# Who multiplies the second layer's attention probabilities by their reciprocal sums: ScalarE or VectorE

## The reference, cut to what matters

```
sc = (q_lat . ckv + q_r . k_r) * HEAD_DIM ** -0.5
sc = where(valid, sc, -inf)
p  = softmax(sc)                    # exp(sc - max) / sum(exp(sc - max))
o_lat = p . ckv ;  o = o_lat . w_uv
out = concat(o) @ w_out
```

## Time and profile before

| | |
|---|---|
| median of three executions | 1579.65 us (1578.85 to 1582.76) |
| the profiled execution | 1582.23 us, its span 1580.4 us |
| PE busy | 1498.1 us (95%) |
| DVE busy | 1279.8 us (81%) |
| ACT busy | 1038.9 us (66%) |
| POOL busy | 113.9 us (7%) |
| mean granted clock of TensorE | 0.981 of full |

### The profile page before, as it was taken

One profiled execution on the slowest core, in us unless ns is written; L12 is line 12 of the kernel. 1 busy time (PEld: TensorE's weight loads), 2 busy tenths in 40 slices (PEclk: granted clock), 3 DMA queues, 4 the chain that ended last, 5 costly groups with the idle time before them and its releaser, 6 DMA issues.

```text
span 1580.4 us, 21687 instructions
## 1 busy us (share of the span) xinstructions
PE 1498.1 (95%) x7201; PEld 1164.0 (74%) x7202; DVE 1279.8 (81%) x1744; ACT 1038.9 (66%) x1357; POOL 113.9 (7%) x112
## 2 busy tenths in 40 slices
PE   3999999999898899999999999999999999999987
PEld 1645468888795478878888888888888888888865
DVE  6896458885584159989989989989989989989987
ACT  3104443443457548787887887888788788788775
POOL 5251000000000000001001001001001001001030
PEclk9999999999799899999999999999999999999999
DMA  9733967874564359999999999999999999999960
GB/s 311 267 107 137 386 253 289 318 247 172 170 214 160 107 218 395 388 347 376 385 349 380 392 353 373 393 352 374 381 370 366 386 362 368 379 371 367 391 241 28
DMA packets 209930, 482.81 MB, mean 305 GB/s; under 512 B 8084, under 2 KB 14534, under 8 KB 209750
## 3 DMA queue, kind: packets, MB, share of 16 engines
q1 hardware_dynamic: 205872, 468.91, 80.7%
q0 software_dynamic: 3360, 12.10, 2.1%
q10 hardware_dynamic: 646, 1.16, 0.2%
HBM read 474.27 MB, written 7.86 MB: 305 GB/s over the span
## 4 chain that ended last, share of the span: by engine, by line
PE 81%; ACT 5%; DVE 5%; issue 2%; DVEq 0%; ACTq 0%
PE ps L864 23%; PE ps L866 22%; PE ps L865 22%; PE ps L870 3%; DVE w_lo L2058 3%; PE ps L1399 2%; PE ps L1156 2%; ACT work L1949 1%; PE ps L1036 1%; PE ps L889 1%; ACT uT L1699 1%; ACT w_hi L1686 1%; PE ps L1067 1%; ACT uT L1708 1%; PE ps L1127 0%
## 5 line engine op out<-in xcount | busy, mean ns | idle before, releaser
L2058 DVE TENSOR_TENSOR w_lo<-ring,w_hi 128x1024 fp32r<-128x1024 f32 (+2 forms) x572 | 675.9, 1214 | 84.8 <-ACT w_hi L1686 63.7
L1686 ACT ACTIVATE w_hi<-ring 128x1024 fp32r<-128x1024 f32 (+2 forms) x572 | 595.9, 1051 | 225.4 <-PE ps L866 222.5
L864 PE MATMUL ps<-w_hi,e_hi 128*128 128x512 f32 x896 | 356.3, 398 | 5.5 <-DVE w_lo L2058 5.5
L866 PE MATMUL ps<-w_hi,e_lo 128*128 128x512 f32 x896 | 349.5, 390 | 0.0
L865 PE MATMUL ps<-w_lo,e_hi 128*128 128x512 f32 x896 | 348.8, 389 | 0.0
L2058 DVE TENSOR_TENSOR w_lo<-ring_more,w_hi 128x1024 fp32r<-128x1024 f32 x192 | 232.1, 1223 | 16.0 <-ACT w_hi L1686 7.0
L1686 ACT ACTIVATE w_hi<-ring_more 128x1024 fp32r<-128x1024 f32 x192 | 202.8, 1060 | 47.5 <-PE ps L866 47.5
L864 PEld LDWEIGHTS ps<-w_hi,e_hi 128*128 128x128 f32 x896 | 168.3, 188 | 42.0 <-DVE w_lo L2058 9.6
L866 PEld LDWEIGHTS ps<-w_hi,e_lo 128*128 128x128 f32 x896 | 168.1, 188 | 36.2
L865 PEld LDWEIGHTS ps<-w_lo,e_hi 128*128 128x128 f32 x896 | 168.5, 188 | 32.8
L864 PE MATMUL ps<-w_hi,eT_hi 128*128 128x512 f32 x448 | 176.7, 395 | 11.9 <-DVE w_lo L2058 11.9
(11 more groups left out here) (306 smaller groups left out, 1593.2 us busy)
## 6 DMA issues: line engine op xcount, KB each, us to landing
ring<-in_moe_w_gate SPq DMA_DIRECT2D x96, 1024.0 KB, 7.0
ring<-in_moe_w_up SPq DMA_DIRECT2D x80, 1024.0 KB, 6.9
ring<-in_moe_w_down SPq DMA_DIRECT2D x64, 1024.0 KB, 7.0
ring<-in_w_ada SPq DMA_DIRECT2D x24, 2048.0 KB, 12.5
ring_more<-in_moe_w_down SPq DMA_DIRECT2D x48, 1024.0 KB, 7.3
ring_more<-in_moe_w_up SPq DMA_DIRECT2D x32, 1024.0 KB, 7.5
ring_more<-in_moe_w_gate SPq DMA_DIRECT2D x16, 1024.0 KB, 7.3
ring<-in_ff_w_gate SPq DMA_DIRECT2D x5, 2048.0 KB, 7.8
```

What stands on the lines that cost most here:

```text
L864: mm(o, xh, wh, start=start, stop=False)
L866: return mm(o, xl, wh, start=False, stop=stop)
L1686: fn(w, src, ACT.Copy).then_inc(hi_ready, 1)
L2058: V.tensor_tensor(w_lo[0:n, c, 0:f], src, w_hi[0:n, c, 0:f].bitcast(F32), ALU.subtract).then_inc(lo_ready, 1)
```

## The change

`probs` is no longer called in layer 1, so ACT issues its four ACTIVATE per pair no more. Instead `weights_sum(n, True)` on DVE waits for its own reciprocal, multiplies the head's two tiles in place by the two reciprocals (`tensor_scalar`), and lets PE go itself (`p_ready`). Nobody waits for `rden_ready` in layer 1 any more. Layer 0 keeps its form.

```
@@ ACT, loop over layer 1's pairs
             for pair in range(C_HEADS // 2):
                 n = A_HEADS + 2 * pair
-                probs(n)
-                probs(n + 1)
                 if pair % 2 == 0:
                     part_out(12 + pair // 2, parts2[:, pair // 2 % 2, :], 6, (0, 0, 13, 14)[pair // 2])
                 probsT_out(n)
@@ DVE, weights_sum(n, l1)
-                V.reciprocal(rden, den).then_inc(rden_ready, 1)
+                if not l1:
+                    V.reciprocal(rden, den).then_inc(rden_ready, 1)
+                else:
+                    chained(V.reciprocal(rden, den))
+                    q = n % 3
+                    for t in range(NT):
+                        x = sm[:, q, KOFF[t]:KOFF[t] + KEYS[t]]
+                        w = V.tensor_scalar(x, x, stat[:, 24 + 2 * q + t:25 + 2 * q + t], None, ALU.mult)
+                        if t < NT - 1:
+                            step(w)
+                    w.then_inc(p_ready, 1)
```

## The result

The changed kernel took 1569.47 us (median of 4, 1568.10 to 1570.98) and the kernel before, run beside it, 1580.43 us (median of 4, 1578.85 to 1582.76). The ratio is 0.9924, 95% interval 0.9909 to 0.9938. The direction and the mechanism of the hand-over between the engines were right, the size was wrong. The profile of the changed kernel is of its fastest execution of the four (1568.10 us); the other three have none.

The account below looks back on a forecast made before the run. Bound: the ACT-PE hand-over in layer 1's attention, with ACT's multiplications a link. Terms 3.18 + 1.25 + 0.24 + 0.24 = 4.91 us; with pair 6, 5.15 to 6.58, set at 5.9: 1579.65 - 5.9 = 1573.8 us, range 1570.0 to 1577.3.

Parts of the forecast that it names:

- pair 0: Layer 1's first pair of heads, ACT the chain: from 5.64 us to 4.39, a gain of 1.25 us.
- pair 1: Layer 1 pair without a matrix-vector product: from 4.26 us to 3.66, a gain of 0.60 us.
- pairs 3, 5, 7 (order alone): Layer 1 pairs where ACT also copies a finished pair of heads: from 4.52 us to 3.66, 0.86 us each.
- pair 2: Layer 1 pair with a matrix-vector product: the small product's wait for ACT's copy goes, a gain of 0.24 us.
- pair 4: Layer 1 pair with a matrix-vector product: taken to gain the same 0.24 us as pair 2.
- pair 6: Low clock in this layer 1 pair, 524.2 to 528.0 us: 1.67 us gained if it goes, 0 if it stays.
- the price on DVE: Per head in layer 1: multiplication starts 0.20 us after the reciprocal's start, two multiplications span 0.55 us.
- The second low-clock stretch goes too: Rival, chance 0.15: low clock at pair 7's end and the product's head also vanishes, some 2.6 us; gain 9.2, time 1570.5.
- The 0.24 goes: In pair 2, the small product L903's 0.24 us wait for ACT's copy L1628 disappears; same taken for pair 4.
- Cover for what is added: DVE's next mask and maximum, pushed by 0.58 us to 3.43, stay hidden: ACT asks at 3.66, 0.23 us spare.

Follow-up runs that it names:

- the filler in the kernel before: Kernel before, ACT still multiplying, with five unused 128x128 matmuls in PE's idle time in each odd pair: ratio 0.9959, median 1578.05 us.
- The second and third profiles: Changed kernel run two more times with no edit: ratios 0.9932 and 0.9938, medians 1573.92 and 1573.27 us.
- the matrix-vector steps: Changed kernel with four steps of the next matrix-vector product moved into pairs 1, 3, 5, ahead of the first transposes: ratio 0.9928, median 1570.77 us.
- The last version: Changed kernel with four matrix-vector steps moved into pairs 1, 3, 5 and seven unused matmuls in pair 7: ratio 0.9899, median 1566.87 us.
- half on each engine: Changed kernel with each pair's first head multiplied on DVE and the second on ACT again: ratio 0.9966, median 1575.79 us.

## Why the prediction was wrong in size

Its sum, term by term, with the profiles' values, in us:

```
term                         predicted   measured
pair 0                          1.25       1.38
pair 1                          0.60       0.60
pairs 3, 5, 7 (order alone)     2.58       2.58
pair 2                          0.24       0.51
pair 4                          0.24       0.58
pair 6                       0 to 1.67     1.63  (0.57 order, 1.06 clock)
pair 7 and product, clock       0          2.49  (first profile; in the other two the stretch was there)
```

*Right.* ACT's multiplications were the link, the price on DVE was 0.20 + 0.55 per head, the odd pairs and their 3.66 us came out exactly, the head copy fell into ACT's wait, and everything behind the attention moved along unchanged. The fall of the clock in pair 6 went, as chosen.

*First failed step: "The second low-clock stretch goes too" was given 0.15 and put at nothing in the sum; it measured 2.49 us.* I argued that PE still idles between four bursts in the last pair, much as before. In the profile that stands beside the median it was gone, 1.03 us in pair 7 and 1.46 in the product, and the filler in the kernel before shows that this time is indeed the clock's, not the order's. The second and third profiles have it again. The case was neither in nor out; it should have had about half of the weight. The range reached a gain of 9.65 us (1579.65 to 1570.0), just short of the 9.77 that the stages give with it, and the measured 11.0 lies another 1.2 us beyond, which no stage holds. The choice of 5.9 halfway between 5.15 and 6.58 took 0.7 us more off a fall in pair 6 that did go.

*Second: pairs 2, 4 and 6 were mis-sized.* "The 0.24 goes" took the idle time printed before L903 as all that the wait cost. It cost 0.51 to 0.58: the row's idle time is counted from the end of the transposes, which PE overlaps with the next operation when nothing holds it (0.38 from start to start, not 0.55). In pair 4 the printed idle time was not 0.24 either but 0.34, which the prediction did not look up. Pair 0 was off by 0.13 in the same way, with operations added up at their printed lengths (0.93 from the scores to the transposes, where the trace has 0.86). Together 0.27 + 0.34 + 0.13 = 0.74, and 0.57 in pair 6 at equal clock.

*Third: the base.* The prediction subtracted from a median of three, 1579.65. Four later sets of the kernel before have medians 1583.28, 1582.02, 1582.23 and 1582.21, and the changed kernel's later medians are 1573.92 and 1573.27, beside the predicted 1573.8. That the time looks close there is luck, two errors of opposite sign: the gain, not the time, is what the steps were about.

*Cover for what is added.* The maxima were in time for ACT, as worked out, but not for PE: in pair 1 PE's scores wait 0.42 us for them. The prediction named only ACT as the one that asks. It cost nothing until the matrix-vector steps filled PE's spare time there.

*What stays open.* The ratios often give more than the stages. The stages give the changed kernel 9.8 us in its first profile and 7.1 in the other two; the ratios give 12.0, 10.8 and 9.8 us of some 1582, with intervals from 6.5 to 14.4 taken together. The last version has 16.0 (13.3 to 18.8) where its stages give 11.8. But the kernel before with filler has such a surplus too, 6.5 against 3.5, though no multiplication moved there, and over the twelve profiles of the table other than the kernel before's own two the surplus goes from -1.0 us (half on each engine) to about +4 (the last version). Each profile is one execution, the ratios go by medians, and the executions of one kernel differ by up to 8 us. So this part is not shown to belong to the change. The clock spell between 396 and 440 us is the largest scatter in the profiles, and nothing here ties it to the edit, whose code comes later.

What in the last pair decides whether the clock falls was not found either: PE's waits up to it are the same with the fall and without. The filler kept it up in three profiles of three (one of them of the kernel before). Without filler it held in four of the nine profiles of kernels in the new order.

## What to carry to other kernels

Choose the engine for a small operation by the stage's busy times and by who waits for its result, not by shares of the whole span (the Trainium skill's page "Perfetto Trace Analysis", section on optimizing Scalar and DVE operations, makes it depend on whether DVE is saturated; here DVE was busy 81% of the span and a third of this stage, and the stage decided). With half of the work moved, pairs 2, 4 and 6 had the whole gain, the odd pairs lacked 0.24 us each and pair 0 lacked 1.03: ask for each operation what waits behind it. Then price the clock as a term of its own: if shortening a wait of PE could lift a low-clock stretch, fill the wait in the kernel before with unused matmuls and read what the clock alone is worth; here it was 3.5 of 9.8 us by the stages. A wait's cost is the difference of start-to-start times with and without it, not the idle time printed at it.

## What the runs showed of the hardware that I had not expected

A matrix-vector product whose matmuls take turns on four column groups of PE (the 128*32 shape) can't be cut just anywhere: 16 matmuls (eight steps) took 1.92 us in one piece, 8 took 1.06, and 4 still 1.05. A cut between groups of four steps costs little; the two steps cut off inside a group cost as much as a full group of four.

Five to seven 128x128 matmuls of the identity in PE's idle times, results unused, kept the granted clock at 1.00 in three profiles of three, through stretches that fell to between 0.50 and 0.58 for 4 to 8 us in both profiles of the kernel before and in two of the three of the changed kernel, and delayed no pair by more than 0.01 us where the same pair exists without them at full clock.
